# Where the rounded weights begin in SBUF: a two-layer attention kernel in float32r

## What is computed

```python
for layer in range(DEPTH):                       # 2 layers
    u = rmsnorm(h, mix_pre_g[layer])
    if layer % 2 == 0:                           # MLA and block attention, 8 heads each
        proj = u @ ab_w_in[e]
        ...
        mixed = jnp.concatenate([mla_out, moba_out], axis=-1) @ ab_w_out[e]
    else:                                        # stick-breaking attention, 16 heads
        qkv = (u @ sb_w_qkv[o]).reshape(B, S, 3, SB_HEADS, HEAD_DIM)
        mixed = stick_breaking_attention(...) @ sb_w_out[o]
    h = h + rmsnorm(mixed, mix_post_g[layer])
    u = rmsnorm(h, ffn_pre_g[layer])
    gu = u @ ffn_w_gate_up[layer]                # 1024 x 5632
    f = (jax.nn.silu(gu[..., :D_FF]) * gu[..., D_FF:]) @ ffn_w_down[layer]   # 2816 x 1024
    h = h + rmsnorm(f, ffn_post_g[layer])
```

## The kernel before, in words

| operand | begins, modulo 512 bytes |
|---|---|
| `hidden`, `so`, `oA`, `probsT`, `v` | 128 |
| `oB`, `cq`, `ckv`, and q and k of the first layer's attention | 256 |
| `u_hi`, `u_lo`, `w_raw`, `w_hi`, `w_lo`, constant matrices | 256 |
| `moba_q5` (one pair of heads; it lies behind the constants) | 32 |

## Time and profile before

### The profile page before, as it was taken

The page is one execution under the profiler, slowest core; times in us unless marked ns, Lnnn a source line. Parts: engine busy times, 40 slices in busy tenths (PEclk is TensorE's granted clock), DMA queues, the critical chain, the costliest instruction groups (busy, mean ns, idle before and its releaser), DMA issues.

```text
span 1338.4 us, 17696 instructions
## 1 busy us (share of the span) xinstructions
PE 1297.8 (97%) x6599; PEld 1092.2 (82%) x6599; DVE 734.4 (55%) x998; ACT 554.5 (41%) x885; POOL 260.2 (19%) x205
## 2 busy tenths in 40 slices
PE   6979999999999999999999999999999999999997
PEld 5667788898888888888898888887988888887885
DVE  4777655538645445422288788686575544553223
ACT  4466666546322332222364555464453222322112
POOL 0532200025211111000051111321431111110002
PEclk8999999999999999999999999999999999999999
DMA  4412222122333333333222111311223333332331
GB/s 158 128 49 64 72 72 71 48 79 80 110 97 101 101 94 92 89 98 94 84 75 68 48 48 55 87 48 48 80 86 104 94 94 98 100 115 79 95 95 63
DMA packets 190503, 112.34 MB, mean 84 GB/s; under 512 B 13696, under 2 KB 184773, under 8 KB 190446
## 3 DMA queue, kind: packets, MB, share of 16 engines
q1 hardware_dynamic: 188636, 106.81, 27.5%
q0 software_dynamic: 640, 2.10, 0.6%
q10 hardware_dynamic: 1170, 2.66, 0.5%
HBM read 109.43 MB, written 4.74 MB: 85 GB/s over the span
## 4 chain that ended last, share of the span: by engine, by line
PE 85%; DVE 8%; ACT 3%; issue 2%; POOL 1%; DMA 0%; POOLq 0%; ACTq 0%; SPq 0%; DVEq 0%
PE banks L432 26%; PE banks L434 25%; PE banks L433 25%; PE banks L1711 3%; DVE w_lo L427 1%; PE banks L1741 1%; PE banks L1629 1%; PE banks L1458 1%; DVE logits L1420 1%; PE banks L481 1%; DVE tf L701 1%; ACT logits L1431 1%; DVE probsT_lo L1470 1%; POOL stick_lo L1728 0%; DVE u_lo L711 0%
## 5 line engine op out<-in xcount | busy, mean ns | idle before, releaser
L427 DVE TENSOR_TENSOR w_lo<-w_raw,w_hi 128x1024 fp32r<-128x1024 f32 (+3 forms) x200 | 288.2, 1444 | 270.7 <-ACT w_hi L420 270.4
L432 PE MATMUL banks<-u_hi,w_hi 128*128 128x512 f32 (+1 forms) x1112 | 425.5, 383 | 5.8 <-DVE w_lo L427 4.3
L434 PE MATMUL banks<-u_hi,w_lo 128*128 128x512 f32 (+1 forms) x1112 | 419.5, 377 | 0.0
L433 PE MATMUL banks<-u_lo,w_hi 128*128 128x512 f32 (+1 forms) x1112 | 419.2, 377 | 0.0
L420 ACT ACTIVATE w_hi<-w_raw 128x1024 fp32r<-128x1024 f32 (+3 forms) x200 | 206.1, 1031 | 282.6 <-PE banks L434 282.5
L432 PEld LDWEIGHTS banks<-u_hi,w_hi 128*128 128x128 f32 x1112 | 210.6, 189 | 45.8 <-issue 4.9
L434 PEld LDWEIGHTS banks<-u_hi,w_lo 128*128 128x128 f32 x1112 | 210.3, 189 | 38.9
L433 PEld LDWEIGHTS banks<-u_lo,w_hi 128*128 128x128 f32 x1112 | 210.5, 189 | 38.0 <-issue 1.0
L904 POOL TENSOR_TENSOR up<-up,gate 128x512 f32<-128x512 f32 x44 | 71.9, 1635 | 375.1 <-DVE up L930 358.3
L885 ACT ACTIVATE gate<-gate 128x512 f32<-128x512 f32 x44 | 27.8, 632 | 202.2 <-DVE gate L926 202.2
L1728 POOL TENSOR_TENSOR stick_lo<-softplus,stick_hi 128x1280 fp32r<-128x1280 f32 x14 | 44.1, 3162 | 157.0 <-DVE stick_hi L1724 157.0
(11 more groups left out here) (256 smaller groups left out, 1983.1 us busy)
## 6 DMA issues: line engine op xcount, KB each, us to landing
w_raw<-in_ffn_w_gate_up_dram SPq DMA_DIRECT2D x88, 512.0 KB, 3.7
w_raw<-in_ffn_w_down_dram SPq DMA_DIRECT2D x30, 512.0 KB, 3.6
w_raw<-in_sb_w_qkv_dram SPq DMA_DIRECT2D x24, 512.0 KB, 3.8
w_raw<-in_ab_w_in_dram SPq DMA_DIRECT2D x17, 512.0 KB, 3.7
w_raw<-in_ffn_w_down_dram SPq DMA_DIRECT2D x16, 448.0 KB, 3.6
w_raw<-in_ab_w_out_dram SPq DMA_DIRECT2D x8, 512.0 KB, 3.9
w_raw<-in_sb_w_out_dram SPq DMA_DIRECT2D x8, 512.0 KB, 4.7
bias_by_distance<-bias_rows ACTq DMA_DIRECT2D x1, 2560.0 KB
```

Source lines behind the costliest of these rows:

```text
L427: dve.tensor_tensor(wl[:, c.slot, 0:w], raw[:, c.slot, 0:w], wh[:, c.slot, 0:w].bitcast(F32), ALU.subtract).then_inc(w_lo, 1)
L432: nc.tensor.matmul(o, lh, rh, start=start, stop=False, skip_group_check=True)
L433: nc.tensor.matmul(o, lh, rl, start=False, stop=False, skip_group_check=True)
L434: return nc.tensor.matmul(o, ll, rh, start=False, stop=stop, skip_group_check=True)
```

## The change

One unnamed tensor of 32 values (128 bytes) is declared ahead of the stage buffers, and `stage_buffers` is 288 values shorter. Stage buffers then begin at 16640, which is 256 modulo 512 (and `oB` and the latents, 128 further, at 384); `residual`, `u` and `w_raw` lie 1024 bytes lower and keep their residue of 256. `w_hi` and `w_lo` are each 3200 values instead of 3072, and the three slots begin at 4, 1032 and 2096 values in them: 16, 32 and 192 bytes modulo 512 behind 256. The constants behind `w_lo` stay where they were. Every use of `wh[:, c.slot, x]` becomes `wh[c.slot][:, x]`, likewise `wl`; the computation, its order and its waits are the same.

```diff
 NSLOT = 3
+SLOT_AT = (4, 1032, 2096)
 AHEAD = 2
...
+        sb(ctx, "stage_line_pad", [P, 32])
         with ExitStack() as at0:
             vh = sb(at0, "v_hi", [P, 2, TT, 192], F32R)
...
-        sb(ctx, "stage_buffers", [P, 27680])
+        sb(ctx, "stage_buffers", [P, 27392])
...
         raw = sb(ctx, "w_raw", [P, NSLOT, 1024])
-        wh = sb(ctx, "w_hi", [P, NSLOT, 1024], F32R)
-        wl = sb(ctx, "w_lo", [P, NSLOT, 1024], F32R)
+        wh_all = sb(ctx, "w_hi", [P, 3200], F32R)
+        wl_all = sb(ctx, "w_lo", [P, 3200], F32R)
+        wh = [wh_all[:, at:at + 1024] for at in SLOT_AT]
+        wl = [wl_all[:, at:at + 1024] for at in SLOT_AT]
...
-            act.activation(wh[:, c.slot, 0:w], raw[:, c.slot, 0:w], ACT.Copy).then_inc(w_hi, 1)
+            act.activation(wh[c.slot][:, 0:w], raw[:, c.slot, 0:w], ACT.Copy).then_inc(w_hi, 1)
...
-            dve.tensor_tensor(wl[:, c.slot, 0:w], raw[:, c.slot, 0:w], wh[:, c.slot, 0:w].bitcast(F32),
+            dve.tensor_tensor(wl[c.slot][:, 0:w], raw[:, c.slot, 0:w], wh[c.slot][:, 0:w].bitcast(F32),
                               ALU.subtract).then_inc(w_lo, 1)
...
-                last = mm3(o, wh[:, c.slot, s], wl[:, c.slot, s], xh[:, first + k, :], xl[:, first + k, :],
+                last = mm3(o, wh[c.slot][:, s], wl[c.slot][:, s], xh[:, first + k, :], xl[:, first + k, :],
                            start=(first + k == 0), stop=(first + k == total - 1))
```

More of the change, by code:

```diff
@@ L571, in f_pe @@
                     xh, xl = operands(pe, at)
-                    last = mm3(bank(b), wh[:, c.slot, s], wl[:, c.slot, s], xh, xl,
+                    last = mm3(bank(b), wh[c.slot][:, s], wl[c.slot][:, s], xh, xl,
                                start=(at == 0), stop=(at == total - 1))
@@ L630, in out_part @@
                 s = slice(k * P, (k + 1) * P)
-                last = mm3(bank(OUT_BANKS[ch][n]), wh[:, c.slot, s], wl[:, c.slot, s], *o_at(k),
+                last = mm3(bank(OUT_BANKS[ch][n]), wh[c.slot][:, s], wl[c.slot][:, s], *o_at(k),
                            start=(k == 0), stop=(k == KD - 1))
@@ L640, in half_products @@
                 xh, xl = o_at(at + k)
-                mm = mm3(bank(b)[:, half(h)], wh[:, c.slot, s], wl[:, c.slot, s], xh[:, half(h)], xl[:, half(h)],
+                mm = mm3(bank(b)[:, half(h)], wh[c.slot][:, s], wl[c.slot][:, s], xh[:, half(h)], xl[:, half(h)],
                          start=(at + k == 0), stop=(at + k == total - 1))
@@ L784, in tile @@
                 s = slice(kk * P, (kk + 1) * P)
-                return mm3(bank(bs[n])[:, half(h)], wh[:, cs3[n].slot, s], wl[:, cs3[n].slot, s],
+                return mm3(bank(bs[n])[:, half(h)], wh[cs3[n].slot][:, s], wl[cs3[n].slot][:, s],
                            uh[:, kk, half(h)], ul[:, kk, half(h)],
@@ L824, in two_products @@
                 for cc, b in ((c, b0), (c.later(1), b1)):
-                    mm = mm3(bank(b), wh[:, cc.slot, s], wl[:, cc.slot, s], uh[:, k, :], ul[:, k, :],
+                    mm = mm3(bank(b), wh[cc.slot][:, s], wl[cc.slot][:, s], uh[:, k, :], ul[:, k, :],
                              start=(k == 0), stop=(k == KD - 1))
@@ L1066, in products @@
                 tok, cols = slice(t * P, (t + 1) * P), slice(half * T, (half + 1) * T)
-                return mm3(bank(b), hidh[:, k, tok], hidl[:, k, tok], wh[:, c.slot, cols], wl[:, c.slot, cols],
+                return mm3(bank(b), hidh[:, k, tok], hidl[:, k, tok], wh[c.slot][:, cols], wl[c.slot][:, cols],
                            start=(k == 0), stop=(k == KF - 1))
```

## The result

The changed kernel takes 1349.03 us, the median of four runs (1348.47 to 1349.24), beside 1338.54 us for the kernel before (four runs): a ratio of 1.0072, with a 95% interval of 1.0060 to 1.0084, or 8 to 11 us. The forecast was 1317.4 us, faster; the time lies on the other side, near the slower rival's 1354.5.

The account below looks back on a forecast made before the run. TensorE's matmul spacing was taken as the bound; u -12.8 and +5.6, hidden -4.2 and -0.2, last projection -4.4, so and oA -1.5, half width -3.5 sum to -21.0 us from 1338.4: 1317.4 us, range 1294 to 1358.

Parts of the forecast that it names:

- the slower rival: Weight products: distances 16, 32 and 192 cost what 128 costs, u pays +16.7 us; 1354.5 us, chance 0.34.
- Part 1: Stage buffers move by 128 bytes: hidden, so and oA reach distance 0 and 226.7 ns, together -7.2 us if alone.
- Part 2, the slots at 16 and 32 bytes: Weight slots: full-width products there run at 220 ns; for u, 1920 x -6.7 ns = -12.8 us.
- The grid of 6.67 ns: Steady spacings fit steps of 6.67 ns, 64 bytes of moving stream: 226.7 is 34 steps, 120.0 is 18, 233.3 is 35.
- The estimate of 217 ns: Unhindered spacing of 512-column products, from eight bf16 matmuls; every weight product today pays 10 to 17 ns on top.
- the row of moba_q5: Product of 64 rows, stationary operand at 32 modulo 512: 1.35 us against 1.37 at 128; taken as 32 bytes doing no harm.
- Part 2, hidden, so, oA and the last projection: Their products in the moved slots: hidden -4.2 and -0.2 us, last projection -4.4, so and oA -1.5.
- The slot at 192: Weight slot at 192 bytes: 232.5 ns, taken from rows at 128 and -128; u +5.6 us, hidden moving -0.2.
- Half width: Products of 256 columns: 113.3 ns in the slots at 16 and 32 bytes, 520 x -6.7 ns = -3.5 us.
- Part 3: Splits of w_hi by ScalarE and w_lo by VectorE write and read at new places: costed at nothing.
- Every distance but 0 is bad: Rival, slower: 1354.5 us, chance 0.34; decides where the three slots' mean for 512 columns is above about 228.5 ns.
- The two outcomes built on it: Forecast of 1317.4 us, chance 0.32, and all three slots reaching 220 ns, 1298.9 us, chance 0.18.

Follow-up runs that it names:

- the bursts: Kernel of products alone, without the model: 72 products per burst, each burst at one distance of weights from moving operand; 226.6 ns at distance 0, 233.4 at 32.

## Why the prediction was wrong

**What bounds the kernel: right.** TensorE's spacing sets the time, and only that; each run's time follows from the number of matmuls in its stretches, and the other engines' busy times moved by 2 us at most. That span and median before agree, which the prediction took as a check, was then chance: the executions that have both figures took some 1.7 us more than their spans. The sum starts at the median and loses nothing by it.

**Part 1: right, 7.2 us forecast and 7.2 measured alone.** Hidden moving and the last projection run at 226.5 and 226.3 ns at distance 0, where 226.7 was forecast, and bring 3.1 and 2.9 us of it (3.2 and 3.0 forecast); so and oA come to 228.2 ns by the starts. In the changed kernel it could not pay, as the slower rival said: nothing is at 0 any more.

**Part 2, the slots at 16 and 32 bytes: the step that failed.** The prediction took "the next step of the grid under 226.7, 33 steps or 220 ns". Measured: 233.1 ns at 32, 230.1 at 16. For the 1920 products with u that is 960 x 5.9 + 960 x 2.9 = +8.4 us in place of -12.8, 21 us apart and most of the miss. Three supports gave way. The grid of 6.67 ns was read from three steady values; the runs with fewer columns and the 228.9, 230.0 and 231.7 ns of the bursts don't lie on it. The estimate of 217 ns, taken from bf16 rows, holds for bf16 (215.7 ns) and not for float32r, whose lowest value over all places tried is 226.6. The reason given with it, that a shift inside 64 bytes could take one step away, is borne out by no shift tried with 512 columns. And the row of moba_q5, nine products of 64 rows, said nothing of the settled spacing at 32.

**Part 2, hidden, so, oA and the last projection.** At 16 and 32, hidden moving stays at 233.2 where 220 was forecast: 0 instead of -4.2 us; the last projection +0.1 instead of -4.4; so and oA -0.3 instead of -1.5.

**The slot at 192: the size was off, in the other direction.** 232.5 ns was taken from the distances of 128; measured 229.4, so u pays 960 x 2.2 = 2.1 us instead of 5.6, and hidden moving gains 3.9 ns a product instead of 1.2.

**Half width: right in sign, small in size.** 113.3 ns was forecast for the slots at 16 and 32, and came at 192 instead, and there with hidden alone; the rest runs at 118. -1.2 us in place of -3.5.

**Part 3, the splits at nothing: right.** In 400 to 540 us the split of w_lo takes 1793 ns (before 1772) and that of w_hi 1054 (before 1053), and TensorE's waits for w_lo come to 6.5 us in six, before 6.6.

**The rival that came.** "Every distance but 0 is bad" has the right kind and the right test: the three slots' mean for u is 230.9 ns, above its 228.5. Its 1354.5 us is 5.5 too high, because 192 costs 229.4 instead of 232.5, every other chunk at 16 runs at 227, and half width gained a little. What spoke for it stood in the prediction: the rows at distance 0 had one constant step, and the down projection's alternated. That was an observation of these very products. The step to 220 ns was an extrapolation from a fitted grid to a value that no row had. The two outcomes built on it got 0.50 together, this rival 0.34; with the weight the other way round the forecast would have been slower.

## What to carry to other kernels

Where matmuls follow each other without a break, count them in a stretch for each pair of operands before the shape is taken for the cost. In float32r with 512 columns, let the moving tiles and the stationary tiles begin at the same address modulo 256 bytes (in all runs here a multiple of 256); in this kernel that is a shift of one region by 128 bytes and 7.2 us, and moving the weights away costs 10.9. A value better than every steady row of the trace is no forecast until a row shows it: scan it by itself, at the length of the real stretch.

## What was not expected of the hardware

- float32r products with a weight load each (128 x 128, 512 columns) run at 226.6 ns at best over all places tried, bf16 at 215.7, same shape and clock; in bf16 four distances make no difference, in float32r the place is worth up to 10 ns (226.6 to 237.0).
- The period is 256 bytes. 512 columns are best at 0 and 240; 256 columns have 113.2 ns at 64 in bursts, and mostly 118.3 at the same place in the kernel.
- At 16 bytes products with the same SBUF addresses run at 226.6 or at 233.2 ns, for a whole burst or chunk. What chooses is open; neither the PSUM bank alone nor the slot ahead does.
- A shorter weight load (188, 134 and 109 ns) made the spacing longer at distance 0 (226.6, 230.0 and 231.7 ns) and shorter at 128 (232.2, 231.2 and 230.7). Why the place of the two reads matters at all is not shown by any of these runs.
